# A hybrid encoder step on one core: the last convolution tile's copies on two queues, the parameters turned first, one split moved

## The chip, the cores and the metric

One core of a Trainium2 chip runs the whole step as one program. The metric is the device time in microseconds; a program is run several times and the median counts. The trace and its page come from one profiled execution.

## The reference, cut to what matters

One inference step of two layers over 512 prompt frames and 32 frames of a running stream, 1024 channels, float32. Layer 0 mixes by attention and gated linear attention, layer 1 by a convolution module, and each is followed by a squared-ReLU MLP behind its own RMSNorm:

```
h = rms_norm(x, norm_mix_g[0]) @ w_in_ab        # 3088 columns: q, k, v, two gates, rank-16 part
x = x + merge(attention(h), gla(h)) @ w_out_ab
x = x + square(relu(rms_norm(x, norm_ffn_g[0]) @ w_up)) @ w_down
u = rms_norm(x, norm_mix_g[1]) @ c_w_pw1 + b1   # 2048 columns
u = u[..., :1024] * sigmoid(u[..., 1024:])      # gated
y = depthwise_conv(u, width 31, causal, per channel) + b_dw
x = x + silu(layer_norm(y)) @ c_w_pw2 + b2
x = x + square(relu(rms_norm(x, norm_ffn_g[1]) @ w_up)) @ w_down
```

The outputs are x and the new caches (keys, values, states, the last 30 gated frames).

## The kernel before

**Layout.** Activations lie with channels on the partitions, eight tiles k of 128 channels by 544 frames. Every projection is cut into units of 256 output columns; unit u reads its 1 MB of weights into one of two buffers, `w_raw[:, u % 2]`. Products are made nearly exact in float32 from halves: ScalarE rounds the weights to `w_h` (L608, `split_hi`), VectorE takes the rest `w_l = w_raw - w_h` (L1514, `split_lo`), and the same is done to x (`x_h`, L637 or L676; `x_l`, L1536 or L1547). TensorE adds w_h x_h, w_h x_l and w_l x_h: 96 matmuls of 128x272 a unit (L1017 in `tile`, L1040 in `together`, L1056 in `by_halves`), into two PSUM slots of two banks each.

**Queues.** Each engine has its own instruction stream, in the order written, and semaphores between them. SP issues all weights: unit u + 2's are asked for as soon as `w_lo` says that unit u is split (L416). GpSimd issues the copies and saves of the middle of the kernel. ScalarE issues two small loads at the start (the norm gains).

**Start.** SP sends x (five transfers, L383 and L384), both first units' weights (L410) and 22 small parameter loads (`load_parameters`, L390 to L404), which all count up `rows_landed`. Among these are `dw_rows` (31 rows of 4 KB, the convolution's weights), six pieces `dw_cross` (6 rows each, the same weights with quarters of their channels turned round) and `cc_rows` (30 rows of 4 KB). TensorE turns x, tile after tile, through four PSUM buffers (L996), which VectorE and ScalarE copy out (L1568, L661; semaphores `x_copied`). Then it runs unit 0 of the input projection in `together` as x_l comes in (with a small turning, L1138, before tile 6), then `parameters()`: it waits for all the parameter loads and turns them, 25 small transposes (L1077 to L1085). VectorE copies them out and spreads them (L1579 to L1591) behind unit 0's scaling (L1609). From unit 2 on, VectorE's norms of q and k set the pace.

**Norm ahead of the convolution.** ScalarE's `norm(2, X_MIX1)` takes the square root (L643) and rounds x (L676); after it comes `split_hi(U_PW1, 0, 1)`, the second gated unit's weights (L608), and then the first gate (L894).

**Convolution.** Eight gated units make eight tiles of `glu`, one each (VectorE, L1912). A tile's 31 taps are shared: VectorE does 11 of them (7 for the last tile, L1929 to L1936), TensorE 20 (24 for the last), as diagonal 32x32 matmuls (`taps`, L1398) in five rounds (six for the last) that read the tile and three copies of it, turned round by 32, 64 and 96 partitions: `glu_rot`. GpSimd makes each copy by two DMAs (L579, L580), six a tile, once the tile is gated (`slot_free[1]`), and `moved[m % 2]` counts them. VectorE adds TensorE's sums (L1961) to its own. For the last tile TensorE first adds the mean of tiles 0 to 3 (`add_mean`, L1414), then does `taps(7)`. ScalarE has by then split the first unit of the second pointwise convolution (U_PW2) and loads its square-root table.

**Keeping the clock.** `keep_clock(n, bank)` (L980) issues n matmuls of 128x256 on ones, whose result nobody reads.

Of the kernel before, what the change touches and what calls it, by code (L numbers as in the profile page):

```python
# [84 lines left out]
def hybrid_kernel(nc, x_prompt, x_sample, cache_a_k, cache_a_v, state_b, cache_c, norm_mix_g, norm_ffn_g,  # L85
# [150 lines left out]
    def width(c):  # L236
# [7 lines left out]
    w_hi, w_lo = sem("w_hi"), sem("w_lo")  # L244
    consts, ones_ready = sem("consts"), sem("ones_ready")
    gains_T, gains_ready = sem("gains_T"), sem("gains_ready")
    r_ready, x_sums, r_rows, r_spread, r_T = (
        sem(n) for n in ("r_ready", "x_sums", "r_rows", "r_spread", "r_T"))

    x_copied = [sem(f"x_copied{n}") for n in range(4)]  # L250
    vec_T = sem("vec_T")
    vec_ready = sem("vec_ready")
    gemm_done = sem("gemm_done")
# [125 lines left out]
    @block.sync  # L379
    def _(sp):  # L380
        xp = x_prompt[0].rearrange("(c p) d -> c p d", p=P)
        for c in range(TT):
            sp.dma_start(x_rows[:, c, :], xp[c]).then_inc(x_landed[c], 16)  # L383
        sp.dma_start(x_rows[0:DEC, TT, :], x_sample[0]).then_inc(x_landed[TT], 16)  # L384

        def load_parameters():
            for at, n, src in ((V_B1, 16, as_rows(c_b_pw1)), (V_BDW, 8, as_rows(c_b_dw)), (V_LNG, 8, as_rows(c_ln_g)),
                               (V_LNB, 8, as_rows(c_ln_b)), (V_B2, 8, as_rows(c_b_pw2)), (V_GB, 2, as_rows(b_gate_b)),
                               (V_ON, 1, b_out_norm_g)):
                sp.dma_start(vec_rows[at:at + n, :], src).then_inc(rows_landed, 16)  # L390
            for at, src in ((V_QG, a_q_norm_g), (V_KG, a_k_norm_g)):
                for b in range(2):
                    sp.dma_start(vec_rows[at:at + 1, b * DA:(b + 1) * DA], src).then_inc(rows_landed, 16)
            sp.dma_start(wlr[:], w_view(w_in_ab[0])[:, :, N_PROJ * P:N_PROJ * P + RANK]).then_inc(rows_landed, 16)
# [7 lines left out]
            sp.dma_start(gate_w[:], b_gate_w_up[0]).then_inc(rows_landed, 16)  # L402
            sp.dma_start(rel, a_rel_bias[0]).then_inc(rows_landed, 16)
            sp.dma_start(state_s[:], state_b[0, 0].rearrange("(a b) k v -> (b k) a v", b=2)).then_inc(rows_landed, 16)  # L404

        def stream(u0, units, source, first=False):

            if first:
                for s in range(2):
                    sp.dma_start(w_raw[:, s], source(s)).then_inc(w_landed[s], 16)  # L410
                load_parameters()
            with sp.Fori(1 if first else 0, units // 2) as i:
                for s in range(2):

                    sp.wait_ge(w_lo, i * 2 + (u0 + s - 1))
                    sp.dma_start(w_raw[:, s], source(i * 2 + s)).then_inc(w_landed[s], 16)  # L416
# [12 lines left out]

        sp.wait_ge(pairs_done, 10)  # L430
        stream(U_OUT, 4, columns(w_out_ab[0]))
        ffn(0, U_FFN0)

        stream(U_PW1, 8, columns(c_w_pw1[0]))
        stream(U_PW2, 4, columns(c_w_pw2[0]))
        ffn(1, U_FFN1)

        yp = y_prompt[0].rearrange("(c p) d -> p c d", p=P)
        for k in range(KT):
            sp.wait_ge(y_stage, 2 * (k + 1))  # L440
# [8 lines left out]
    def _(pool):  # L449
# [123 lines left out]
        for m in range(KT):  # L573

            pool.wait_ge(slot_free[1], m + (tile0(U_PW1) // 2 + 1))
            pool.wait_ge(taps_done, m + 1)
            for j in range(1, ROTS):
                at = P - j * (P // ROTS)
                pool.dma_start(glu_rot[0:at, m % 2, j - 1, :], glu[P - at:P, m, 0:PAD + SEQ]).then_inc(moved[m % 2], 16)  # L579
                pool.dma_start(glu_rot[at:P, m % 2, j - 1, :], glu[0:P - at, m, 0:PAD + SEQ]).then_inc(moved[m % 2], 16)  # L580

        pool.wait_ge(edges_out, 2)
        pool.dma_start(cc_prompt[0, 0], ccn[0]).then_inc(stored, 16)
# [6 lines left out]
    def _(act):  # L590
# [6 lines left out]

        for at, src in ((V_MIX, norm_mix_g), (V_FFN, norm_ffn_g)):
            act.dma_start(vec_rows[at:at + 16, :], as_rows(src)).then_inc(gains_landed, 16)

        def split_hi(u, i, d):

# [50 lines left out]
        act.activation(no_use[:], eps[:], ACT.Sqrt)  # L653
        act.wait_ge(gains_ready, 1)
        for k in range(KT):
            hi_gain(0, x_h, k, V_MIX, x_copied[k % 4], k // 4 + 1)
            if k == 1:
                split_hi(0, 0, 0)
                for late in (6, 7):
                    act.wait_ge(gemm_done, late + 1)  # L660
                    act.activation(resid[:, late, :], flat(late % 4)[:, 0:TOK], ACT.Copy).then_inc(x_copied[late % 4], 1)  # L661
                    act.wait_ge(x_copied[late % 4], 2)
        for n, c in enumerate((3, 4)):
            if n:

# [218 lines left out]
                    last(u)  # L884

        ffn(0, U_FFN0, lambda u: phase(u, 4, squares_of(2, u)))
        norm(2, X_MIX1)


# [16 lines left out]

        act.wait_ge(glu_edges, 7)

        split_hi(U_PW1, 0, 1)
        with act.Fori(0, KT // 2 - 1) as i:  # L910
            for s in range(2):
                gate(i, s)
# [7 lines left out]
        gate(KT // 2 - 1, 1)  # L920

        split_hi(U_PW2, 0, 1)
        act.activation(no_use[:], eps[:], ACT.Sqrt)

        def cv_deviation(c):
# [47 lines left out]
    def _(pe):  # L973
# [12 lines left out]
        pe.transpose(ps[:, 4, 0:V_B1], vec_rows[0:V_B1, :], ident[0:V_B1, 0:V_B1]).then_inc(gains_T, 1)  # L986
        pe.wait_ge(gains_ready, 1)
        for k in range(KT):
            if k >= 4:
                pe.wait_ge(x_copied[k % 4], 1)  # L990
            for c in range(TT + 1):
                if k == 0:
                    keep_clock((0, 14, 6, 2, 2)[c], 6)
                    pe.wait_ge(x_landed[c], 16)
                M = width(c)
                ins = pe.transpose(flat(k % 4)[:, c * P:c * P + M], x_rows[0:M, c, k * P:(k + 1) * P],  # L996
                                   ident[0:M, 0:M])
            ins.then_inc(gemm_done, 1)

# [73 lines left out]


        def parameters():
            pe.wait_ge(rows_landed, 16 * 23)
            pe.transpose(ps[:, 7, 0:V_N], vec_rows[:], ident[0:V_N, 0:V_N]).then_inc(vec_T, 1)  # L1077
            for k in range(KT):
                ins = pe.transpose(ps[:, 7, V_N + k * CONV:V_N + (k + 1) * CONV], dw_rows[:, k * P:(k + 1) * P], ident[0:CONV, 0:CONV])
# [52 lines left out]
        def x_ready(k):  # L1132
            if k == KT - 2:

                pe.wait_ge(r_spread, 1)
                for c in range(TT + 1):
                    M = width(c)
# [1 line left out]
                ins.then_inc(r_T, 1)  # L1139
            pe.wait_ge(xl_ready, X_MIX0 + k + 1)  # L1140

        for n in range(4):
            pe.wait_ge(x_copied[n], 2)
        together(0, 0, x_h, x_l, x_ready)
        parameters()
        for u in range(1, U_ATT - 1):
            if u == 2:
                pe.wait_ge(vec_ready, 1)
# [234 lines left out]
        def taps(m):  # L1383
# [4 lines left out]
            pe.wait_ge(moved[s], (m // 2 + 1) * 96)  # L1388

            if m:  # L1390
                pe.wait_ge(conv_step, m * STEPS)
# [86 lines left out]
    def _(dve):  # L1478
# [86 lines left out]

        for k in range(KT - 2):
            dve.wait_ge(gemm_done, k + 1)
            dve.tensor_copy(resid[:, k, :], flat(k % 4)[:, 0:TOK]).then_inc(x_copied[k % 4], 1)  # L1568
        split_lo(0, 0, 0)
        for k in range(KT):  # L1570
            dve.wait_ge(x_copied[k % 4], k // 4 + 1)
            lo_gain(k, X_MIX0, x_l, x_h, V_MIX)
            if k == KT - 3:
                dve.wait_ge(std_ready, 1)
# [2 lines left out]
        def parameters():  # L1577
# [5 lines left out]
            dve.tensor_copy(w_dw[:].rearrange("p k c -> p (k c)"), ps[:, 7, V_N:V_N + KT * CONV])  # L1583
            dve.tensor_copy(dw_rot[:].rearrange("p k c -> p (k c)"), ps[:, 7, V_N + KT * CONV:V_N + KT * (CONV + CROSS)])
            dve.wait_ge(vec_T, 3)
            dve.tensor_copy(cc_T[:].rearrange("p k c -> p (k c)"), ps[:, 6, 0:KT * PAD]).then_inc(vec_ready, 1)

            near = 384 + NREL - 1
# [47 lines left out]
        for u in range(U_ATT):  # L1636
# [3 lines left out]
                copy_rows(3)  # L1640
            split_lo(0, 0, u + 1)
            if u == 0:
                dve.wait_ge(r_ready, 1)
            for m in range(2):
                if 2 <= u < 6:
# [433 lines left out]
```

## Time and profile before

| | us |
|---|---|
| median of 3 runs (lowest, highest) | 1371.54 (1370.0, 1373.36) |
| the profiled execution | 1374.85 |
| its span, first to last instruction | 1373.1 |
| TensorE busy | 1344.9 (98%) |
| VectorE busy | 703.2 (51%) |
| ScalarE busy | 472.7 (34%) |
| mean granted clock of TensorE | 0.993 of full |
| its chain of work, share of TensorE | 90% |

The span is that of the engines' instructions, the execution's time has some 1.75 us around it. TensorE's busy time includes slow matmuls and those of `keep_clock`, so 98% busy does not mean that all of it is needed. A row of the timeline gives the start, the duration, the engine (PE is TensorE, PEld its weight loads, DVE VectorE, ACT ScalarE, POOL GpSimd; a q behind the name is the engine's queue of issues), the line, and in brackets how long the engine stood idle before it and who released it.

### The profile page before, as it was taken

The numbers are of one execution on the slowest core, as the hardware profiler recorded it, in microseconds if no ns is written. First come the engines' busy times: TensorE is split into PE (matmuls) and PEld (weight loads), VectorE is DVE, ScalarE is ACT, GpSimd is POOL, SyncE is SP. The second block draws the span as 40 slices with busy tenths as digits, with TensorE's granted clock in tenths as the row PEclk, the third lists the DMA queues.
The fourth block names the chain that finished last, engine by engine and source line by source line (L and its number), as shares of the span: only waits on it lengthen the run. The fifth ranks groups of instructions, "written<-read, shape, count | busy, mean of one in ns | idle before, by whom it ended". The sixth has DMA issues, their size and how long they took to land.

```text
span 1373.1 us, 27650 instructions
## 1 busy us (share of the span) xinstructions
PE 1344.9 (98%) x11649; PEld 1274.7 (93%) x11649; DVE 703.2 (51%) x1028; ACT 472.7 (34%) x792; POOL 86.5 (6%) x145
## 2 busy tenths in 40 slices
PE   8999999999999999999999999989999999999998
PEld 7998888779999999999999888858999999999998
DVE  5693568575544334334324788877544334334322
ACT  4221556434333223123122544445433223223111
POOL 4001100001100000000011111101100000000000
PEclk9999999999999999999999999999999999999999
DMA  7223300222222222222221433302222221222221
GB/s 253 80 92 106 119 27 2 95 72 93 82 83 82 92 92 92 92 85 74 96 84 62 112 110 106 104 16 69 93 93 92 93 92 61 95 90 92 92 78 50
DMA packets 107293, 119.90 MB, mean 87 GB/s; under 512 B 4435, under 2 KB 103358, under 8 KB 106943
## 3 DMA queue, kind: packets, MB, share of 16 engines
q1 hardware_dynamic: 102783, 101.50, 23.1%
q0 software_dynamic: 4352, 17.02, 4.2%
q8 instruction: 72, 1.18, 0.3%
q14 instruction: 22, 0.18, 0.0%
q10 hardware_dynamic: 64, 0.02, 0.0%
HBM read 104.66 MB, written 7.21 MB: 81 GB/s over the span
## 4 chain that ended last, share of the span: by engine, by line
PE 90%; DVE 5%; ACT 2%; issue 2%; DMA 1%; POOL 0%; SPq 0%; DVEq 0%; ACTq 0%; POOLq 0%
PE ps L1017 70%; PE ps L1173 4%; PE ps L1398 3%; PE ps L1040 3%; DVE rstd L1613 2%; PE ps L1190 1%; PE ps L1284 1%; PE ps L980 1%; PE ps L1223 1%; PE ps L1207 1%; PE ps L1056 1%; PE ps L1002 1%; DVE w_l L1514 1%; PE ps L1438 1%; DMA x_rows<-in_x_sample 1%
## 5 line engine op out<-in xcount | busy, mean ns | idle before, releaser
L608 ACT ACTIVATE w_h<-w_raw 128x2048 fp32r<-128x2048 f32 x92 | 175.4, 1907 | 276.4 <-PE ps L1017 272.9
L1514 DVE TENSOR_TENSOR w_l<-w_raw,w_h 128x2048 fp32r<-128x2048 f32 x92 | 210.8, 2291 | 102.8 <-ACT w_h L608 102.7
L1017 PE MATMUL ps<-x_h,w_h 128*128 128x272 f32 x1152 | 242.0, 292 | 2.4 <-ACT sig L894 1.5
L1017 PE MATMUL ps<-x_l,w_h 128*128 128x272 f32 x1152 | 238.6, 288 | 0.0
L1017 PE MATMUL ps<-x_h,w_l 128*128 128x272 f32 x1152 | 238.2, 288 | 0.0
L1017 PE MATMUL ps<-xf_h,w_h 128*128 128x272 f32 x1024 | 212.9, 289 | 0.0
L1017 PE MATMUL ps<-xf_l,w_h 128*128 128x272 f32 x1024 | 211.2, 287 | 0.0
L1017 PE MATMUL ps<-xf_h,w_l 128*128 128x272 f32 x1024 | 210.9, 287 | 0.0
L1017 PEld LDWEIGHTS ps<-x_h,w_h 128*128 128x128 f32 x1152 | 180.9, 189 | 9.1 <-issue 8.7
L1017 PEld LDWEIGHTS ps<-x_l,w_h 128*128 128x128 f32 x1152 | 182.6, 189 | 0.0
L1017 PEld LDWEIGHTS ps<-x_h,w_l 128*128 128x128 f32 x1152 | 180.7, 188 | 0.0
L1017 PEld LDWEIGHTS ps<-xf_l,w_h 128*128 128x128 f32 x1024 | 161.5, 188 | 0.0
L1017 PEld LDWEIGHTS ps<-xf_h,w_h 128*128 128x128 f32 x1024 | 159.9, 188 | 0.2
L1017 PEld LDWEIGHTS ps<-xf_h,w_l 128*128 128x128 f32 x1024 | 159.8, 188 | 0.0
L1861 DVE TENSOR_TENSOR resid<-ps,resid 128x544 f32 x64 | 46.3, 724 | 200.6 <-PE ps L1017 199.7
L870 ACT ACTIVATE relu<-relu 128x544 f32<-128x544 f32 x64 | 42.2, 659 | 239.9 <-DVE relu L1879 239.9
L1017 PE MATMUL ps<-odd_h,w_h 128*128 128x272 f32 x512 | 106.8, 290 | 0.0
L1017 PE MATMUL ps<-odd_l,w_h 128*128 128x272 f32 x512 | 105.6, 287 | 0.0
L1017 PE MATMUL ps<-odd_h,w_l 128*128 128x272 f32 x512 | 105.5, 287 | 0.0
L1879 DVE SCALAR_TENSOR_TENSOR relu<-ps,xn 128x544 f32<-128x544 f32 x64 | 46.2, 722 | 89.6 <-PE ps L1017 89.5
L1017 PEld LDWEIGHTS ps<-odd_l,w_h 128*128 128x128 f32 x512 | 80.8, 188 | 0.0
L1017 PEld LDWEIGHTS ps<-odd_h,w_l 128*128 128x128 f32 x512 | 79.9, 188 | 0.0
(278 smaller groups left out, 1653.5 us busy)
## 6 DMA issues: line engine op xcount, KB each, us to landing
w_raw<-in_w_ffn_up SPq DMA_DIRECT2D x32, 1024.0 KB, 5.3
w_raw<-in_w_ffn_down SPq DMA_DIRECT2D x32, 1024.0 KB, 5.1
w_raw<-in_w_in_ab SPq DMA_DIRECT2D x12, 1024.0 KB, 5.3
w_raw<-in_c_w_pw SPq DMA_DIRECT2D x12, 1024.0 KB, 6.1
w_raw<-in_w_out_ab SPq DMA_DIRECT2D x4, 1024.0 KB, 5.5
glu_rot<-glu POOLq DMA_DIRECT2D x16, 203.2 KB, 5.4
resid_scratch<-resid POOLq DMA_DIRECT2D x1, 2176.0 KB, 8.1
resid<-resid_scratch POOLq DMA_DIRECT2D x1, 2176.0 KB, 9.0
```

The lines of the kernel that those rows point to most:

```text
L608: act.activation(w_h[s][:], w_raw[:, s], ACT.Copy).then_inc(w_hi, 1)
L870: act.activation(relu2[:, m, :], relu[:, m, :], ACT.Square).then_inc(relu2_done, 1)
L980: pe.matmul(ps[:, bank, 0:2 * P], any_bits[:, 0:P], any_bits, start=True, stop=True)
L1002: ins = pe.matmul(dst[:, a, :], w[:], src[:, a * n:(a + 1) * n], start=start, stop=stop)
L1017: ins = pe.matmul(ps[:, 2 * m + t, 0:HALF], a[s][:, k, w], b[:, k, t * HALF:(t + 1) * HALF], start=(k == 0 and q == 0), stop=(k == KT - 1 ...
L1040: ins = pe.matmul(ps[:, 2 * m + t, 0:HALF], a[s][:, k, w], b[:, k, t * HALF:(t + 1) * HALF], start=(k == 0 and q == 0), stop=(k == KT - 1 ...
L1173: ins = pe.matmul(ps[:, 2 * m + t, 0:HALF], a[u % 2][:, k, m * P:(m + 1) * P], b[:, k, t * HALF:(t + 1) * HALF], start=(k == 0 and q == 0) ...
L1398: ins = pe.matmul(ps[to, 4 + r, :], diag[rows, s, tap, :], src, start=(n == 0), stop=(n == rounds(m) - 1))
L1514: dve.tensor_tensor(w_l[s][:], w_raw[:, s], w_h[s][:].bitcast(F32), ALU.subtract).then_inc(w_lo, 1)
L1613: dve.reciprocal(rstd[:, 0:TOK], sumsq[:]).then_inc(rstd_ready, 1)
L1861: dve.tensor_tensor(r, slot(m), r, ALU.add).then_inc(slot_free[m], 1)
L1879: dve.scalar_tensor_tensor(out=halves(relu[:, m, :]), in0=slot(m), scalar=0.0, in1=halves(r_tok), op0=ALU.max, op1=ALU.mult).then_inc(slot ...
```

## The change

Four things are done:

1. **Last tile's copies.** GpSimd issues only three of the last tile's six copies; ScalarE issues the other three, behind its split of U_PW2's first unit, with their own semaphore `moved_last`. SP's weights for U_PW2 + 2 and the one after wait for all six. TensorE runs eight `keep_clock` matmuls between `add_mean(3)` and `taps(7)`.
2. **Parameters.** The eleven loads of vectors go to ScalarE's queue. SP sends dw_rows, dw_cross and cc_rows between the first and the second unit's weights, and the other four (`load_late_parameters`) behind the second, counted by `late_rows`. TensorE turns the parameters ahead of unit 0, with a wait for 19 loads, and then runs eight `keep_clock` matmuls; VectorE handles them ahead of unit 0's scaling and waits there for the late four.
3. **Three PSUM buffers for x** instead of four, since the parameters' turnings use the last two banks.
4. **Split.** `split_hi(U_PW1, 0, 1)` stands ahead of `norm(2, X_MIX1)`.

```diff
         def load_parameters():
-            for at, n, src in ((V_B1, 16, as_rows(c_b_pw1)), ... (V_ON, 1, b_out_norm_g)):
-                sp.dma_start(vec_rows[at:at + n, :], src).then_inc(rows_landed, 16)
-            (4 more of a_q_norm_g, a_k_norm_g; wlr)
             sp.dma_start(dw_rows[:], c_w_dw[0]).then_inc(rows_landed, 16)
...
             sp.dma_start(cc_rows[:], cache_c[0, 0]).then_inc(rows_landed, 16)
-            (gate_w, rel, state_s)
+        def load_late_parameters():
+            (wlr, gate_w, rel, state_s, each .then_inc(late_rows, 16))
...
                 for s in range(2):
                     sp.dma_start(w_raw[:, s], source(s)).then_inc(w_landed[s], 16)
-                load_parameters()
+                    (load_parameters, load_late_parameters)[s]()
...
-        stream(U_PW2, 4, columns(c_w_pw2[0]))
+        stream(U_PW2, 2, columns(c_w_pw2[0]))
+        sp.wait_ge(moved[(KT - 1) % 2], KT // 2 * 96 - 48)
+        sp.wait_ge(moved_last, 48)
+        stream(U_PW2 + 2, 2, columns(c_w_pw2[0], 512))
...  (GpSimd)
                 pool.dma_start(glu_rot[0:at, ...], glu[P - at:P, m, ...]).then_inc(moved[m % 2], 16)
-                pool.dma_start(glu_rot[at:P, ...], glu[0:P - at, m, ...]).then_inc(moved[m % 2], 16)
+                if m < KT - 1:
+                    pool.dma_start(glu_rot[at:P, ...], glu[0:P - at, m, ...]).then_inc(moved[m % 2], 16)
...  (ScalarE)
+        (at the start: the eleven loads of vec_rows, .then_inc(rows_landed, 16))
-            hi_gain(0, x_h, k, V_MIX, x_copied[k % 4], k // 4 + 1)
+            hi_gain(0, x_h, k, V_MIX, x_copied[k % 3], k // 3 + 1)
...
+        split_hi(U_PW1, 0, 1)
         norm(2, X_MIX1)
         act.wait_ge(glu_edges, 7)
-        split_hi(U_PW1, 0, 1)
...
         split_hi(U_PW2, 0, 1)
+        act.wait_ge(slot_free[1], KT - 1 + (tile0(U_PW1) // 2 + 1))
+        act.wait_ge(taps_done, KT)
+        for j in range(1, ROTS):
+            at = P - j * (P // ROTS)
+            act.dma_start(glu_rot[at:P, (KT - 1) % 2, j - 1, :], glu[0:P - at, KT - 1, 0:PAD + SEQ])\
+                .then_inc(moved_last, 16)
         act.activation(no_use[:], eps[:], ACT.Sqrt)
...  (TensorE)
-            if k >= 4:
-                pe.wait_ge(x_copied[k % 4], 1)
+            if k >= 3:
+                pe.wait_ge(x_copied[k % 3], k // 3)
...
-            pe.wait_ge(rows_landed, 16 * 23)
+            pe.wait_ge(rows_landed, 16 * 19)
...
-        for n in range(4):
-            pe.wait_ge(x_copied[n], 2)
+        parameters()
+        for n in range(2):
+            pe.wait_ge(x_copied[n], 3)
+        keep_clock(8, 0)
         together(0, 0, x_h, x_l, x_ready)
-        parameters()
...
         for k in range(4):
             add_mean(k)
+        pe.wait_ge(slot_free[1], tile0(U_PW2) // 2)
+        keep_clock(8, 2)
         taps(KT - 1)
...  (VectorE)
+            dve.wait_ge(late_rows, 16 * 4)      (in parameters())
...
             if u == 0:
+                parameters()
                 dve.wait_ge(r_ready, 1)
...
-            if u == 0:
-                parameters()
```

## Rows read from the trace of the kernel before

**Rows 1.** The page, chain of work that ended last, by engine.

```profile
PE 90%; DVE 5%; ACT 2%; issue 2%; DMA 1%; POOL 0%; SPq 0%; DVEq 0%; ACTq 0%; POOLq 0%
```

**Rows 2.** Timeline of the start: start us, us, engine, line, operation.

```profile
4.74 5.57 SPq L390 DMA_DIRECT2D vec_rows<-in_c_b_pw  x1
...
13.97 0.43 SPq L395 DMA_DIRECT2D dw_rows<-in_c_w_dw  x1
...
19.25 0.46 SPq L401 DMA_DIRECT2D cc_rows<-in_cache_c  x1
...
11.51 1.44 ACT L637 ACTIVATE x_h<-resid,vecs 128x544 fp32r<-128x544 f32 x2 [8.27 <-DVE resid L1568]
...
13.12 1.91 ACT L608 ACTIVATE w_h<-w_raw 128x2048 fp32r<-128x2048 f32 x1 [0.17 <-DMA w_raw<-in_w_in_ab]
...
18.25 0.61 PE L1040 MATMUL ps<-x_h,w_h 128*128 128x272 f32 x2 [2.28 <-DVE x_l L1536]
```

**Rows 3.** Windows: busy us of each engine, granted clock, DMA share, GB/s.

```profile
18.25:21.83 3.58, 3.58 (x16) 3.58 (x17) 3.33 (x5) 3.55 (x7) 0.00 (x0) 0.53 0.22 68
...
883.70:889.20 5.50, 5.50 (x162) 2.83 (x160) 3.95 (x6) 3.40 (x3) 1.22 (x3) 1.00 0.20 63
...
897.40:902.40 5.00, 4.95 (x96) 2.17 (x97) 1.84 (x3) 0.00 (x0) 0.00 (x0) 0.50 0.00 0
```

**Rows 4.** Chain and VectorE timeline at the ends of units 0 and 1.

```profile
32.90 0.07 PE ps L1077
...
34.58 12.28 PE ps L1017 x96
...
46.88 0.73 DVE L1609 TENSOR_TENSOR proj<-ps,xn 128x544 f32<-128x544 f32 x1 [5.30 <-PE ps L1017]
```

**Rows 5.** Timeline around the last tile's copies and taps.

```profile
887.98 0.52 POOL L579 DMA_DIRECT2D glu_rot<-glu  x1 [14.62 <-DVE glu L1912]
...
890.51 0.52 POOL L580 DMA_DIRECT2D glu_rot<-glu  x1
...
889.22 4.15 PE L1414 MATMUL ps<-cv,mean_d 128*128 128x288 f32 x16
...
897.45 1.08 PE L1398 MATMUL ps<-glu,diag 32*32 32x512 f32 x4 [4.08 <-DMA glu_rot<-glu]
...
906.35 0.69 DVE L1961 TENSOR_TENSOR rstd<-ps,rstd 128x512 f32<-128x512 f32 x1 [7.04 <-PE ps L1398]
...
910.68 1.04 PE L980 MATMUL ps<-ones 128*128 128x256 bf16 x8
```

**Rows 6.** Timeline of the norm ahead of the gated units.

```profile
744.68 0.71 ACT L643 ACTIVATE sumsq<-ps,eps 128x544 f32<-128x544 f32 x1 [2.69 <-PE ps L1002]
...
759.21 1.90 ACT L608 ACTIVATE w_h<-w_raw 128x2048 fp32r<-128x2048 f32 x1
...
765.27 0.49 PE L1017 MATMUL ps<-x_h,w_h 128*128 128x272 f32 x2 [1.52 <-ACT sig L894]
```

**Rows 7.** DMA issues, us to landing: last tile's longest copies, first tile's.

```profile
glu_rot<-glu POOLq DMA_DIRECT2D x2, 203.2 KB, 5.9
...
glu_rot<-glu POOLq DMA_DIRECT2D x2, 203.2 KB, 3.6
```

**Rows 8.** DMA packets in 5:6, 17:18, 22:22.5 and 22.5:23 us.

```profile
DMA packets 107, 0.38 MB, mean 377 GB/s; under 512 B 14, under 2 KB 15, under 8 KB 107
...
DMA packets 60, 0.04 MB, mean 36 GB/s; under 512 B 54, under 2 KB 54, under 8 KB 60
...
DMA packets 57, 0.01 MB, mean 28 GB/s; under 512 B 50, under 2 KB 57, under 8 KB 57
...
DMA packets 134, 0.07 MB, mean 147 GB/s; under 512 B 7, under 2 KB 132, under 8 KB 134
```

**Rows 9.** VectorE timeline: unit 0's scalings, last parameter operation.

```profile
32.25 1.41 DVE L1609 TENSOR_TENSOR proj<-ps,xn 128x544 f32<-128x544 f32 x2 [4.76 <-PE ps L1040]
...
36.14 0.18 DVE L1591 COPY proj<-proj 8x65 f32<-8x65 f32 x1
```

More of the change, by code:

```diff
@@ L246, in hybrid_kernel @@
     gains_T, gains_ready = sem("gains_T"), sem("gains_ready")
+    moved_last = sem("moved_last")
+    late_rows = sem("late_rows")
     r_ready, x_sums, r_rows, r_spread, r_T = (
         sem(n) for n in ("r_ready", "x_sums", "r_rows", "r_spread", "r_T"))
-    x_copied = [sem(f"x_copied{n}") for n in range(4)]
+    x_copied = [sem(f"x_copied{n}") for n in range(3)]
     vec_T = sem("vec_T")
@@ L386, in load_parameters @@
         def load_parameters():
-            for at, n, src in ((V_B1, 16, as_rows(c_b_pw1)), (V_BDW, 8, as_rows(c_b_dw)), (V_LNG, 8, as_rows(c_ln_g)),
-                               (V_LNB, 8, as_rows(c_ln_b)), (V_B2, 8, as_rows(c_b_pw2)), (V_GB, 2, as_rows(b_gate_b)),
-                               (V_ON, 1, b_out_norm_g)):
-                sp.dma_start(vec_rows[at:at + n, :], src).then_inc(rows_landed, 16)
[L391 to L394, printed above, removed]
             sp.dma_start(dw_rows[:], c_w_dw[0]).then_inc(rows_landed, 16)
@@ L401, in load_parameters @@
             sp.dma_start(cc_rows[:], cache_c[0, 0]).then_inc(rows_landed, 16)
-            sp.dma_start(gate_w[:], b_gate_w_up[0]).then_inc(rows_landed, 16)
-            sp.dma_start(rel, a_rel_bias[0]).then_inc(rows_landed, 16)
-            sp.dma_start(state_s[:], state_b[0, 0].rearrange("(a b) k v -> (b k) a v", b=2)).then_inc(rows_landed, 16)
+        def load_late_parameters():
+            sp.dma_start(wlr[:], w_view(w_in_ab[0])[:, :, N_PROJ * P:N_PROJ * P + RANK]).then_inc(late_rows, 16)
+            sp.dma_start(gate_w[:], b_gate_w_up[0]).then_inc(late_rows, 16)
+            sp.dma_start(rel, a_rel_bias[0]).then_inc(late_rows, 16)
+            sp.dma_start(state_s[:], state_b[0, 0].rearrange("(a b) k v -> (b k) a v", b=2)).then_inc(late_rows, 16)
         def stream(u0, units, source, first=False):
@@ L579, in _ @@
                 pool.dma_start(glu_rot[0:at, m % 2, j - 1, :], glu[P - at:P, m, 0:PAD + SEQ]).then_inc(moved[m % 2], 16)
-                pool.dma_start(glu_rot[at:P, m % 2, j - 1, :], glu[0:P - at, m, 0:PAD + SEQ]).then_inc(moved[m % 2], 16)
+                if m < KT - 1:
+                    pool.dma_start(glu_rot[at:P, m % 2, j - 1, :], glu[0:P - at, m, 0:PAD + SEQ])\
+                        .then_inc(moved[m % 2], 16)
         pool.wait_ge(edges_out, 2)
@@ L599, in _ @@
             act.dma_start(vec_rows[at:at + 16, :], as_rows(src)).then_inc(gains_landed, 16)
+        for at, n, src in ((V_B1, 16, as_rows(c_b_pw1)), (V_BDW, 8, as_rows(c_b_dw)), (V_LNG, 8, as_rows(c_ln_g)),
+                           (V_LNB, 8, as_rows(c_ln_b)), (V_B2, 8, as_rows(c_b_pw2)), (V_GB, 2, as_rows(b_gate_b)),
+                           (V_ON, 1, b_out_norm_g)):
+            act.dma_start(vec_rows[at:at + n, :], src).then_inc(rows_landed, 16)
+        for at, src in ((V_QG, a_q_norm_g), (V_KG, a_k_norm_g)):
+            for b in range(2):
+                act.dma_start(vec_rows[at:at + 1, b * DA:(b + 1) * DA], src).then_inc(rows_landed, 16)
         def split_hi(u, i, d):
@@ L660, in _ @@
                     act.wait_ge(gemm_done, late + 1)
-                    act.activation(resid[:, late, :], flat(late % 4)[:, 0:TOK], ACT.Copy).then_inc(x_copied[late % 4], 1)
-                    act.wait_ge(x_copied[late % 4], 2)
+                    act.activation(resid[:, late, :], flat(late % 3)[:, 0:TOK], ACT.Copy).then_inc(x_copied[late % 3], 1)
+                    act.wait_ge(x_copied[late % 3], 3)
         for n, c in enumerate((3, 4)):
@@ L995, in _ @@
                 M = width(c)
-                ins = pe.transpose(flat(k % 4)[:, c * P:c * P + M], x_rows[0:M, c, k * P:(k + 1) * P],
+                ins = pe.transpose(flat(k % 3)[:, c * P:c * P + M], x_rows[0:M, c, k * P:(k + 1) * P],
                                    ident[0:M, 0:M])
@@ L1133, in x_ready @@
             if k == KT - 2:
+                pe.wait_ge(x_copied[2], 2)
                 pe.wait_ge(r_spread, 1)
@@ L1387, in taps @@
             pe.wait_ge(slot_free[1], m + (tile0(U_PW1) // 2 + 1))
-            pe.wait_ge(moved[s], (m // 2 + 1) * 96)
+            if m < KT - 1:
+                pe.wait_ge(moved[s], (m // 2 + 1) * 96)
+            else:
+                pe.wait_ge(moved[s], (m // 2 + 1) * 96 - 48)
+                pe.wait_ge(moved_last, 48)
             if m:
@@ L1567, in _ @@
             dve.wait_ge(gemm_done, k + 1)
-            dve.tensor_copy(resid[:, k, :], flat(k % 4)[:, 0:TOK]).then_inc(x_copied[k % 4], 1)
+            dve.tensor_copy(resid[:, k, :], flat(k % 3)[:, 0:TOK]).then_inc(x_copied[k % 3], 1)
         split_lo(0, 0, 0)
         for k in range(KT):
-            dve.wait_ge(x_copied[k % 4], k // 4 + 1)
+            dve.wait_ge(x_copied[k % 3], k // 3 + 1)
             lo_gain(k, X_MIX0, x_l, x_h, V_MIX)
@@ L1585, in parameters @@
             dve.wait_ge(vec_T, 3)
+            dve.wait_ge(late_rows, 16 * 4)
             dve.tensor_copy(cc_T[:].rearrange("p k c -> p (k c)"), ps[:, 6, 0:KT * PAD]).then_inc(vec_ready, 1)
```

## The prediction

> **What bounds the kernel now.** The page comes first: its chain of work that ended last belongs to TensorE for nine tenths [rows 1]. A microsecond counts here only where TensorE is late for its next dense stretch. The change touches three such places, so I read each in the timeline, engine by engine, and then asked the windows for the granted clock there.
>
> The first is the start. TensorE has turned x by 15.97 us (its next row starts at 18.25 after 2.28 us idle), then waits for VectorE's x_l [rows 2]. It comes back slow: from 18.25 to 21.83 the mean granted clock is 0.53, practically the 1.2 GHz level, and 16 matmuls take 3.58 us [rows 3]; at the full 2.4 GHz, as in unit 1, 96 take 12.28 [rows 4], so 16 would take 2.0. Unit 0 ends at 32.90, the parameters' 25 turnings follow until 34.58, and unit 1 starts [rows 4].
>
> The second is the gap ahead of the last tile's taps. GpSimd issues that tile's six copies from 887.98 on, half a microsecond each; the last was issued at 890.51 and TensorE waited for it until 897.45, 4.08 us idle; its mean work before had ended at 889.22 + 4.15 = 893.37 [rows 5]. The clock fell there too: 0.50 over the 5 us after, and VectorE, which had been done for 7.04 us, got the sums at 906.35 [rows 3, 5].
>
> The third is the norm ahead of the gated units [rows 6].
>
> **The copies.** Before, the 1 MB of a later unit's weights goes out beside them, and the longest copies took 5.9 us to landing; for the first tile, whose copies start almost 3 us behind the weights, the same ones took 3.6 [rows 7]. After, SP holds the weights back until the copies are in, GpSimd issues three copies and ScalarE three. GpSimd's third is issued 2 x 0.52 us behind 887.98, at 889.0; with 3.6 us it lands at 892.6. ScalarE's three start when its unit is gated, about 887.7, and are no later. TensorE has mean work until 893.37 anyway, and then eight clock matmuls, 1.04 us in the row of the same eight [rows 5], 0.95 of it their own: taps can start at 894.3, so the landing has 1.7 us to spare. At full clock five rounds took 5.45 us (the stretch of tile 6 [rows 3]); the last tile has six, 6.54. They end at 900.85, and VectorE starts its sums at 900.95 instead of 906.35: **5.4 us less**, some 3.15 from the start and 2.25 from the clock. VectorE is free at 906.35 - 7.04 = 899.31, 1.6 us ahead, so it does not take over. Bounds: landings of 5.9 us as before give 894.9, 0.6 us lost; 0 more is to be had by faster ones, since the clock matmuls stand in the way. ScalarE's three issues and its table load are covered by its next wait, which ends only behind VectorE's sums. The held weights land near 898, and their unit is split only after unit 0 of this projection, which starts when the whole normalisation is done. Nothing else stands behind SP's two waits: all SP does later is weights.
>
> One rule of the Trainium skill speaks against the second queue (DMA: Bandwidth & Descriptors, "Issuing engines are not separate DMA queues"): all issuers share the same 16 engines, so a second one saves issue time only. The trace agrees that issue time counts (six issues end at 891.03, three at about 889.5), and the sum above takes its gain from that and from the held weights, not from bandwidth.
>
> **The parameters.** Removed: 1.68 us between unit 0 and unit 1 (32.90 to 34.58 [rows 4]). Added: the same turnings ahead of unit 0, a wait for 19 transfers, eight clock matmuls, and three PSUM buffers for x instead of four. The third buffer suffices: a tile's copy runs while the next is turned, so the buffer of three tiles ago is free a tile ahead.
>
> So all hangs on when the 19 transfers are in. Eleven small ones move to ScalarE's queue; at SP's 0.3 to 0.45 us each they cost it about 5 us at the start, where it has 8.27 us idle before 11.51 [rows 2]. The other eight are dw_rows, six pieces of dw_cross and cc_rows. Before, SP gave them out from 13.97 to 19.71, behind both units of weights; SP also stood 5.57 us in the first small one [rows 2]. After, they follow the first unit alone: issued between 4 and 10 us, or by 15 if SP stands likewise. They are then moved behind the first weights, which land at 13.10 (ScalarE's wait [rows 2]). And dw_rows goes slowly: between 17 and 18 us, with nothing else moving, there are 60 packets, 54 of them under 512 B and 6 of 4 KB [rows 8]. While x came in, 92 of 4 KB went over 16 engines in a microsecond (107 less 15) [rows 8]; six is one engine's rate. Its 31 rows are therefore a 31 / 6 = 5.2 us job. Behind them on that engine are its share of dw_cross (50 small packets in the half microsecond from 22.0) and two rows of cc_rows (the two large ones from 22.5 on) [rows 8]: 0.7 + 0.3 us. The landing lag is the same as for the weights, so the rows are in at 13.1 + 6.2 = 19.3; the engine may be done with the weights before the slowest one, and I take **19.0**, against TensorE's 15.97. From below: 18.2, if the engine is free 1.1 us ahead of that landing. From above: 20.4: before, the rows were given out at 13.97 and done by 22.0, so they may have taken up to 1.4 us more than 5.2 behind the second weights.
>
> The Trainium skill has this as a rule (DMA: Bandwidth & Descriptors, "Why a DMA increments its semaphore by 16 and not by 1"): a hardware-issued transfer runs on the largest number of engines up to 16 that divides its outer dimension, and always on the lowest-numbered. For 31 rows that is one; the trace agrees, with its 6 packets a microsecond. Were the rows spread over all sixteen, the sum would be that of rival (a) below.
>
> Against the start at 18.25 that gives: resumption 0.75 us later; eight clock matmuls in front of unit 0, 0.95; the turnings only change place; at the end of unit 0 nothing stands between it and unit 1 any more, which must wait for VectorE's first scaling (0.70 us, begun 0.65 before the end [rows 4, 9]): 0.1. The clock: idle 3.0 us instead of 2.28. 2.28 us idle was followed by 3.58 slow, 4.08 by 5.0 [rows 2, 3, 5], in between 4.2; 0.6 us more at half speed costs 0.25. **Together 2.05 us more** (1.25 to 3.5 with the bounds).
>
> Cover elsewhere: VectorE's share (its last operation ends at 36.32, some 2.2 us behind the turnings it waits for) moves to 27.5, where it had 4.76 us idle [rows 9], if the four late transfers are in by then; they are issued behind the second weights, by about 18, and should land by 24. The second weights lose their early place: behind dw_rows on that one engine they land near 22. Their split on ScalarE and VectorE takes 4.2 us and TensorE needs it at 34 [rows 4]: 8 us to spare, less what VectorE's queue adds. Does the 2.05 us pass through? VectorE waited 5.30 us for unit 1's end at 46.88 [rows 4], and its bound stretch begins from that, so yes.
>
> **The earlier split.** ScalarE had 2.69 us idle before 744.68, the split takes 1.91 and fits with 0.8 to spare. It was at 759.21 and its result is due with the gate, and the gate waits for unit 0 and a table load, not for it: TensorE's 1.52 us of idle are ended by the sigmoid [rows 6]. **0 us**; worst case about 1, should the split push the square root.
>
> **Sum.** -5.4 + 2.05 + 0 = -3.35 us on a profiled execution of 1374.85 (span 1373.1, 1.75 around it). The median shown is 3.3 lower, 1371.54; the same step gives **1368.2**.
>
> **Rivals.** (a) The rows are in before 15.97. Then the turnings fill the gap, the clock never falls, unit 0 starts at 15.97 + 1.68 + 0.95 = 18.6 and ends 13.07 us later (14.65 less 1.58 of slow clock) at 31.7, unit 1 starts at 31.8 instead of 34.58: -2.8, in all -8.2, **1363.3**. For it: the small packets are quick. Against it: one engine needs 5.2 us for dw_rows and can't start before 11. 0.17.
>
> (b) The turnings all run at the lower level, and the slow stretch of 4.2 us only follows, over the clock matmuls and unit 0. The turnings take 1.68 x 0.8 = 1.35 us more: -2.0, **1369.5**. For it: both slow stretches of the rows ended inside long runs of matmuls, none inside turnings. Against it: nothing in the rows says that turnings are different. 0.18.
>
> (c) Slower: the rows land no sooner than before, about 24 (last large packets after 22.5, and the lag), because SP's stand of 5.57 us or the one engine delays them in their new place too. TensorE then stands 8 us: 5.75 + 0.95 + 0.1 + 0.6 of clock = 7.4, less 5.4 = +2.0, **1373.5**. It decides from a landing at 22.3 on. Against it: the packets' order above. 0.08.
>
> (d) The copies still take their 6.7 us: they land at 895.7, taps begin 1.4 us later, gain 4.0: **1369.6**; with the clock lost too, about 1372. 0.12.
>
> My forecast 0.45, on its own 1367 to 1370. 0.3% is 4.1 us, about what this measurement can tell: the forecast stands just inside. Faster by more: (a) and some 0.2 of the forecast (rows by 18.4, or the last bits of the copies): 0.37. Slower by more: 0.08. Within: 0.55. Range: 1363.2, the foot of (a), to 1371.8, above (d).
>
> **What would show it.** Start: TensorE idle from 16 to 19, released by a transfer, clock 0.5 for about 4 us, unit 1 at 36.6. No idle and unit 1 at 31.8 is (a); slow beyond 4 us of dense work is (b); a start after 22.3 is (c). Taps of the last tile: start 8 clock matmuls behind 893.4 in old time, no wait, clock 1.00, 6.5 us long. The norm unchanged but for the split's place. I am wrong if dw_rows does not hold one engine, or if a stage between 47 and 250 us absorbs the start's delay.

## The result, and the profile after

The changed kernel takes 1374.62 us (median of 20 runs, 1373.16 to 1376.08) against 1371.78 for the kernel before on the same chip (20 runs, 1369.17 to 1374.26). The ratio is 1.0019, 95% interval 1.0013 to 1.0026: **slower by 0.2%, 2.6 us**, where 3.3 us less was predicted and the range ended at 1371.8. That is within the 0.3% that counts here as no change, but on the slower side, outside the range. The profiled execution took 1374.62 us (span 1372.9), which is 0.2 less than the profiled execution of before (1374.85). So one profiled execution and the median tell different stories here.

**The start.** First the chain of waits of the kernel after, from 15 to 41 us (start, us, what); it answers to [rows 2, 4].

```profile
10.43 10.03 DMA cc_rows<-in_cache_c
20.46 0.04 issue
20.51 0.40 PE ps L1094
20.91 0.99 PE ps L1096 x8
21.90 0.83 PE ps L1099 x8
22.73 0.87 PE ps L1102 x8
23.61 1.82 PE ps L997 x8
25.43 9.83 PE ps L1057 x72
35.26 0.61 PE ps L1156 x5
35.87 2.48 PE ps L1057 x18
...
38.40 0.47 issue
38.86 0.74 DVE proj L1635
...
39.73 1.37 PE ps L1034 x9
```

and two rows of TensorE's timeline at the end of unit 0:

```profile
38.67 0.41 PE L1057 MATMUL ps<-x_h,w_l 128*128 128x272 f32 x2
39.73 0.49 PE L1034 MATMUL ps<-x_h,w_h 128*128 128x272 f32 x2 [0.65 <-DVE proj L1635]
```

TensorE stands until the last of the 19 transfers is in at 20.46, turns the parameters for 3.1 us (1.68 before), runs eight clock matmuls for 1.82, and starts unit 0 at 25.43. The chain leaves TensorE at 38.35, where the first half of unit 0's result is ready for VectorE; the last matmul of unit 0 ends at 39.08. Unit 1 starts at 39.73, behind VectorE's first scaling, 5.15 us later than in [rows 4]. Three PSUM buffers for x suffice: turning it takes 5.56 us before and after. The windows of the same kernel (busy us of each engine, granted clock, DMA share, GB/s) show the clock from the end of x on:

```profile
16.80:20.50 3.70, 0.00 (x0) 0.00 (x0) 3.70 (x5) 3.61 (x6) 0.00 (x0) 0.96 0.33 65
20.50:23.60 3.10, 3.09 (x26) 2.88 (x27) 1.88 (x3) 3.07 (x6) 0.00 (x0) 0.50 0.56 142
23.60:27.00 3.40, 3.40 (x17) 2.96 (x17) 2.95 (x4) 2.19 (x3) 1.72 (x2) 0.50 0.70 243
27.00:28.00 1.00, 1.00 (x10) 1.00 (x9) 1.00 (x1) 0.00 (x0) 0.15 (x1) 0.98 0.65 279
...
889.45:894.40 4.95, 4.95 (x160) 2.60 (x128) 3.45 (x6) 1.65 (x1) 1.17 (x3) 1.00 0.04 11
899.40:905.90 6.50, 6.50 (x193) 3.65 (x192) 5.09 (x7) 0.00 (x0) 0.00 (x0) 1.00 0.49 164
```

All of the turnings are at 0.50, the 1.2 GHz level, and so are the 3.4 us behind them.

**Why the rows were late.** SP's timeline in the kernel after:

```profile
3.90 0.66 SPq L389 DMA_DIRECT2D dw_rows<-in_c_w_dw  x1
...
10.43 0.76 SPq L395 DMA_DIRECT2D cc_rows<-in_cache_c  x1
11.23 1.76 SPq L407 DMA_DIRECT2D w_raw<-in_w_in_ab  x1
13.04 5.72 SPq L398 DMA_DIRECT2D wlr<-in_w_in_ab  x1
```

SP gave all eight out between 3.90 and 11.2, as predicted; its stand of 5.7 us moved to the first late transfer, where nobody waits for it. What was late is the one engine that works on `dw_rows`: from 13 to 18 us it passed only 4 or 5 packets of 4 KB in each microsecond, where the sum had 6. The DMA packets in 13:14, 15:16 and 18:19:

```profile
DMA packets 41, 0.05 MB, mean 49 GB/s; under 512 B 5, under 2 KB 37, under 8 KB 41
...
DMA packets 346, 0.37 MB, mean 370 GB/s; under 512 B 0, under 2 KB 341, under 8 KB 346
...
DMA packets 40, 0.02 MB, mean 20 GB/s; under 512 B 37, under 2 KB 37, under 8 KB 40
```

The large ones are the last figure less the one before it: 4, 5 and 3. In 15:16 the second unit's weights go beside them, 341 smaller packets on all engines. The last three of `dw_rows` pass between 18 and 18.5, at the 6 a microsecond of the sum; the 37 small ones come behind them, then the two large ones of `cc_rows`. From about 11.6 (11 large packets in 11.5:12, none in 10.5:11.5) to 19.6 us the engine was at it: some 7 us for `dw_rows` and 1 for the rest.

**The copies.** The timeline around the last tile, answering to [rows 5]:

```profile
892.97 1.91 ACTq L938 DMA_DIRECT2D glu_rot<-glu  x3
893.23 1.53 POOL L580 DMA_DIRECT2D glu_rot<-glu  x3 [14.64 <-DVE glu L1937]
894.47 4.15 PE L1437 MATMUL ps<-cv,mean_d 128*128 128x288 f32 x16
...
898.46 1.04 PE L997 MATMUL ps<-ones 128*128 128x256 bf16 x8
...
899.37 0.37 SPq L413 DMA_DIRECT2D w_raw<-in_c_w_pw  x1
...
906.06 0.69 DVE L1986 TENSOR_TENSOR rstd<-ps,rstd 128x512 f32<-128x512 f32 x1 [1.50 <-PE ps L1421]
```

and of the copies (first and last issue; us to landing):

```profile
L938 ACTq DMA_DIRECT2D glu_rot<-glu x3: 616/617/623, 893.0 to 894.3; - x3
...
glu_rot<-glu ACTq DMA_DIRECT2D x1, 203.2 KB, 5.0
```

Mean work, clock matmuls and taps follow each other without a wait, the taps take 6.50 us at clock 1.00, and VectorE gets the sums at 906.06: 13.1 us after the first copy, against 906.35 - 887.98 = 18.4 in [rows 5]. Everything here is 5.25 us late from the start, and still the sums come 0.3 us sooner. The margin is thin: ScalarE's last copy, given out at 894.3, is in at 899.2, 0.6 us behind the end of the mean work and about 0.2 ahead of the taps; the clock matmuls cover that gap. Against that one execution the gain is 906.35 + 5.25 - 906.06 = 5.5 us, where 5.4 was predicted.

### The profile page after: what moved, and what is told of

Its sections match the earlier page's. It is cut to its first block, busy times and chain, and to the rows that moved or that the text cites. A ratio compares the mean times of both kernels' runs of the same rounds, so it can differ in the third digit from the quotient of the medians.

```text
span 1372.9 us, 27674 instructions
## 1 busy us (share of the span) xinstructions
PE 1347.1 (98%) x11665; PEld 1276.1 (93%) x11665; DVE 702.7 (51%) x1028; ACT 472.4 (34%) x792; POOL 84.4 (6%) x142
## 4 chain that ended last, share of the span: by engine, by line
PE 91%; DVE 4%; ACT 2%; issue 1%; DMA 1%; SPq 1%; POOL 0%; ACTq 0%; DVEq 0%; POOLq 0%
PE ps L1034 71%; PE ps L1192 4%; PE ps L1421 3%; PE ps L1057 3%; DVE rstd L1639 2%; PE ps L997 1%; PE ps L1209 1%; PE ps L1303 1%; PE ps L1242 1%; PE ps L1226 1%; PE ps L1019 1%; DMA cc_rows<-in_cache_c 1%; PE ps L1073 1%; DVE w_l L1539 1%; PE ps L1463 1%
```

## The experiments

All ratios are to the kernel before on the same chip. There were eleven runs, two of them of the kernel before itself.

**1. The kernel before again, and each part alone.**

> The kernel before, unchanged, profiled and timed once more. The profiled execution shown took 1374.85 us, above every one of its 20 timed ones (1369.17 to 1374.26, median 1371.78). Theory A (that execution was unlucky: one or both of its slow stretches of TensorE's clock, at 18.25 and 897.45 us, is often absent or shorter): this profile ends 2 to 4 us sooner, and the difference lies in a stretch with granted clock near 0.5, at the start or at the last tile's taps. Theory B (the profile costs some 3 us of its own, everywhere): the profile again takes 1374 to 1375 us and the same stretches are slow. Timed: ratio 1.000 within 0.001 either way.

> Only the last tile's part: three copies issued by ScalarE, later weights held back, eight clock matmuls ahead of the taps. From the two traces this part gives back 5.5 us (unit times 5.2 us later at tile 6, 0.3 earlier at the last tile's sums). If the gap and its slow clock are there in every execution of the kernel before: 5.0 to 5.5 us faster, ratio 0.9960. If the clock falls there only in some executions: about 3.2 to 4.5 us faster, 0.997 to 0.9975.

The copies' part: three of the six copies on ScalarE's queue, two units' weights held back, eight clock matmuls.

> Only the start: parameters' loads reordered and turned ahead of unit 0, three buffers for x, eight clock matmuls. From the two profiled executions: unit 1 starts 5.2 us later (39.7 instead of 34.6), ratio 1.0038. If the start of the kernel before is usually quicker than in the profiled execution (its clock falls at 18.25 only sometimes, worth up to 1.6 us, or x lands sooner), the timed loss is larger: 6 to 8.5 us, 1.0045 to 1.006, since the measured whole is +2.8 and the copies gain at most 5.5.

The parameters' part, with its eight clock matmuls.

> Only the split of the second gated unit's weights moved ahead of the norm. It fills idle time of ScalarE and nobody waits for its result: 0 us, ratio 1.0000 within 0.0007. Rival: it delays the square root or the loads and costs 1 us or more, which would explain part of what the sum of the two traces leaves open.

```diff
+        split_hi(U_PW1, 0, 1)
         norm(2, X_MIX1)
...
-        split_hi(U_PW1, 0, 1)
         with act.Fori(0, KT // 2 - 1) as i:
```

| kernel | median us | ratio, 95% | profiled: us, clock |
|---|---|---|---|
| before again | 1371.22 | 0.9999 [0.9989, 1.0009] | 1372.86, 0.995 |
| copies only | 1368.81 | 0.9980 [0.9971, 0.9989] | 1368.99, 0.996 |
| parameters only | 1377.98 | 1.0052 [1.0039, 1.0065] | 1377.91, 0.994 |
| split only | 1372.42 | 1.0000 [0.9989, 1.0011] | 1374.67, 0.993 |

In us at 1371.9: copies -2.7 (-4.0 to -1.5), parameters +7.1 (5.4 to 8.9), split 0. Their sum, +4.4, is 1.8 above the whole change's, which the three intervals allow. So the copies give half of what was predicted, and the new start costs more than three times as much as predicted.

**2. The rows of the taps in two transfers, and the start without its clock matmuls.** The first of the two edits, made on the parameters' part alone and on the whole change:

```diff
-            sp.dma_start(dw_rows[:], c_w_dw[0]).then_inc(rows_landed, 16)
+            sp.dma_start(dw_rows[0:16], c_w_dw[0, 0:16]).then_inc(rows_landed, 16)
+            sp.dma_start(dw_rows[16:CONV], c_w_dw[0, 16:CONV]).then_inc(rows_landed, 16)
...
-            pe.wait_ge(rows_landed, 16 * 19)
+            pe.wait_ge(rows_landed, 16 * 20)
```

> The start part alone, and dw_rows loaded by two transfers of 16 and 15 rows instead of one of 31. Theory (the 31 rows of 4 KB run on one DMA engine, 0.2 us each, and hold the parameters back until 20.5): now the rows are in at 15 to 16 us, before x is turned at 16.5 to 16.8; the parameters are turned at once, 1.7 us at full clock, TensorE's granted clock does not fall, unit 0 starts near 19.3 and unit 1 near 33 instead of 39.7: 1.5 to 2 us sooner than in the kernel before (34.6 to 35.2), and timed about 2 to 3 us faster than it, ratio 0.998 to 0.9985. Rival (the small pieces of dw_cross or SP's issue times hold the rows): in at 18 to 20 us, unit 1 at 37 to 39, slower than before by 3 us or more.

The second, on the parameters' part alone:

```diff
-        keep_clock(8, 0)
         together(0, 0, x_h, x_l, x_ready)
```

> The start part alone, without its eight clock matmuls ahead of unit 0. They ran at half clock for 1.8 us. If they only stand in the way: unit 0 starts 1.8 us sooner, but the slow stretch of 3.4 us then covers unit 0's matmuls instead, at a cost of 0.9 of it; unit 1 starts 0.9 to 1.0 us sooner (38.8 to 39.0). If they bring the clock back: unit 1 no sooner, within 0.2 us.

> The whole changed kernel with dw_rows in two transfers. The start's gain of 1.5 to 2 us and the copies' 2.7 to 5.5: 4.5 to 7 us faster than the kernel before, ratio 0.995 to 0.9967, and 7 to 10 us faster than the changed kernel. If the rows are not what holds the start: as the changed kernel, 1.002.

| kernel | median us | ratio, 95% |
|---|---|---|
| parameters, rows spread | 1373.26 | 1.0006 [0.9992, 1.0019] |
| parameters, no clock matmuls | 1374.64 | 1.0023 [1.0011, 1.0035] |
| whole change, rows spread | 1368.83 | 0.9968 [0.9953, 0.9982] |

The timeline of TensorE with the rows spread, parameters only:

```profile
17.46 0.29 PE L1083 MATMUL ps<-ident,vec_rows 85*128 85x85 f32 x1 [1.17 <-DMA cc_rows<-in_cache_c]
17.68 0.68 PE L1085 MATMUL ps<-ident,dw_rows 31*128 31x31 f32 x8
...
19.28 1.45 PE L986 MATMUL ps<-ones 128*128 128x256 bf16 x8
20.39 0.80 PE L1046 MATMUL ps<-x_h,w_h 128*128 128x272 f32 x2
```

and in the whole change with the rows spread:

```profile
16.57 0.29 PE L1095 MATMUL ps<-ident,vec_rows 85*128 85x85 f32 x1
...
18.39 1.05 PE L998 MATMUL ps<-ones 128*128 128x256 bf16 x8
19.92 0.48 PE L1058 MATMUL ps<-x_h,w_h 128*128 128x272 f32 x2 [0.48 <-DVE x_l L1562]
```

The same bytes in two transfers of 16 and 15 rows are in 3 us sooner (17.4) or before TensorE asks at all: from 14 us on the first of these kernels has 4 packets of 4 KB left (2 in 14:15, 2 in 15:16), where the kernel after had 23; the rows go 0.68 us through TensorE instead of 1.06, at full clock, and timed 4.6 of the 5.2 thousandths are gone. The rule of the Trainium skill that the prediction used (DMA: Bandwidth & Descriptors, "Why a DMA increments its semaphore by 16 and not by 1") says that the outer dimension sets the number of engines; this experiment changes that dimension, at the price of one transfer more, and the time follows. Without the clock matmuls the late rows stay late, and unit 1 starts at 39.07 instead of 39.90; timed, the step is 1.0052 (five runs) to 1.0023, so these matmuls bring nothing behind a stall of 3.7 us. That they cost more than the 0.8 us of the profile is not shown: the two intervals almost touch. The third kernel beats both: 0.3% faster than before, and 0.5% faster than the change by the ratio of their ratios.

The first kernel missed its expectation: TensorE still waited 1.17 us for the last transfer, the clock fell at 19.8 us for 3.4 us, and unit 1 started at 35.44, not near 33. Timed it is no faster than the kernel before, where 2 to 3 us were expected. The third came out at the slow end of what was expected of it (0.995 to 0.9967).

**3. The two halves of the copies' part, the kernel before a third time, and the best version without the clock matmuls ahead of unit 0.** Queue only keeps ScalarE's three copies and the clock matmuls and drops what holds the weights back (this edit and the next are shown against the changed kernel; start and split are those of before):

```diff
-        stream(U_PW2, 2, columns(c_w_pw2[0]))
-        sp.wait_ge(moved[(KT - 1) % 2], KT // 2 * 96 - 48)
-        sp.wait_ge(moved_last, 48)
-        stream(U_PW2 + 2, 2, columns(c_w_pw2[0], 512))
+        stream(U_PW2, 4, columns(c_w_pw2[0]))
```

> Half of the copies' part: the last tile's six copies on two queues and the eight clock matmuls, the last two units' weights as early as in the kernel before; start and split as before. The whole part gave -2.7 us timed. Theory, that the clock matmuls cover what the weights beside the copies still cost: landings of 5 to 6 us from 888.7 to 889 on end at 894 to 895, mean work ends near 893 and the clock matmuls 1 us later, so the taps wait 0 to 1 us and the clock stays 1.00: 1369 to 1370, ratio 0.998 to 0.999. Rival, that the gain is that of the held weights: landings stay at 6.7 us, taps wait 1.5 us or more and the clock falls: 1371 to 1372.

Hold only leaves all six copies on GpSimd:

```diff
-                if m < KT - 1:
-                    pool.dma_start(glu_rot[at:P, m % 2, j - 1, :], ...)
+                pool.dma_start(glu_rot[at:P, m % 2, j - 1, :], ...)
...
-        sp.wait_ge(moved[(KT - 1) % 2], KT // 2 * 96 - 48)
-        sp.wait_ge(moved_last, 48)
+        sp.wait_ge(moved[(KT - 1) % 2], KT // 2 * 96)
```

> The other half: all six copies stay on GpSimd, the weights of the last two units go out behind them, and the eight clock matmuls stand in front of the taps. The last copy is issued some 2.5 us behind the first, near 890.2, and with 3.6 to 4.5 us it is in at 893.8 to 894.7 against 893.8 to 894 for the end of the clock matmuls: a wait of 0 to 0.9 us, clock 1.00, 1368.8 to 1370. Rival, that the issue time of six on one queue is what costs: wait over 1.5 us, 1371 or more.

> The whole change with the rows of the taps in two transfers of 16 and 15 rows, and without the eight clock matmuls ahead of unit 0 (those ahead of the last tile's taps stay). With them the same kernel gave 1368.83, 0.9968 of the kernel before, and no slow stretch at the start. Theory A, that they only cost their 0.95 us where nothing is waited for: unit 0 starts 0.9 to 1.0 us earlier, the clock stays 1.00, 0.996, near 1368. Rival B, that VectorE's first x_l sets the start of unit 0 (idle of 0.48 us there in that kernel): 0 to 0.5 us earlier, and the gap costs a slow stretch of 3.4 us, which is 1.7 us: 0.997 to 0.998.

> The kernel before once more, for a third profile of it. If its slow stretches around the last tile's copies are the same in every execution: 6.8 us at half clock between 895 and 903 as in the first profile, and 1374 to 1375. If they vary from execution to execution: 3.4 us there as in the second, or another number, and a time of the profiled execution that goes with the slow time in all (13.6 us slow gave 1372.9, 20.5 gave 1374.9). Ratio 0.999 to 1.001.

| kernel | median us | ratio, 95% | profiled: us, clock |
|---|---|---|---|
| queue only | 1372.22 | 1.0005 [0.9990, 1.0020] | 1376.08, 0.991 |
| hold only | 1368.71 | 0.9974 [0.9960, 0.9988] | 1370.89, 0.993 |
| spread, no clock matmuls | 1367.84 | 0.9972 [0.9959, 0.9985] | 1370.85, 0.993 |
| before, third time | 1370.34 | 0.9991 [0.9976, 1.0005] | 1371.42, 0.995 |

The gain of the copies' part comes with the weights that are held back; the second queue adds nothing to it. Both halves have the clock matmuls, so held weights without them are not tested; in hold only the last copy is in 0.6 us behind the mean work, as in the change. DMA issues and their landing (us) with the second queue and the weights beside it:

```profile
glu_rot<-glu POOLq DMA_DIRECT2D x1, 203.2 KB, 6.0
glu_rot<-glu ACTq DMA_DIRECT2D x1, 203.2 KB, 7.7
glu_rot<-glu ACTq DMA_DIRECT2D x1, 135.5 KB, 6.5
...
glu_rot<-glu POOLq DMA_DIRECT2D x1, 67.8 KB, 7.4
```

and with one queue and the weights held back:

```profile
glu_rot<-glu POOLq DMA_DIRECT2D x2, 203.2 KB, 3.0
glu_rot<-glu POOLq DMA_DIRECT2D x2, 135.5 KB, 2.6
glu_rot<-glu POOLq DMA_DIRECT2D x2, 67.8 KB, 2.7
```

The queue-only kernel issues sooner and lands no sooner: its taps start 9.23 us after its first copy, and the seven profiles with the old copies have 8.1 to 9.5. In the hold-only kernel that is 6.2, in the whole part 6.4 to 6.5; both run from mean work through the clock matmuls into the taps without a wait, and both reach the next landmark, VectorE's first split of weights behind the convolution, the same 4.5 us sooner than the second profile of before. So rival "issue time costs" fell, and so did my expectation that queue only would reach 1369 to 1370: the wait was 2.7 us, not 0 to 1. It bears out the rule that was weighed in the prediction (the Trainium skill, DMA: Bandwidth & Descriptors, "Issuing engines are not separate DMA queues"), which calls the issue time that a second queue saves usually small beside the transfer itself; the prediction had held against it that six issues against three count, and they did not.

The clock matmuls ahead of unit 0 can't be told apart from none once the rows are early (0.9968 and 0.9972). Neither theory of that run could be read from its profile, since the clock had fallen at 11.9 us already, ahead of the code that differs. Nor can either be told from hold only (0.9974): with the rows early the new start costs nothing that shows, and what it gains, if anything, is lost in the intervals.

**4. What the clock does when nothing is changed.** Windows of 895.5 to 902.5 us, where the last tile's taps begin, in the second profile of the kernel before:

```profile
895.50:902.50 7.00, 6.26 (x152) 3.64 (x164) 2.81 (x4) 0.00 (x0) 0.00 (x0) 0.76 0.01 2
```

and in the third:

```profile
895.50:902.50 7.00, 6.17 (x192) 3.66 (x192) 3.91 (x6) 0.00 (x0) 0.00 (x0) 1.00 0.02 5
```

The first profile has 0.50 over the same taps [rows 3]. Reading the stages in this way gives the time at half clock, us:

| profile of | start | attention, near 140 | last tile's taps | near 930 |
|---|---|---|---|---|
| before | 3.4 | 6.8 | 6.8 | 3.4 |
| before again | 3.4 | 3.4 | 3.4 | 3.4 |
| before, third | 6.8 | 3.4 | 0 | 3.4 |
| copies only | 3.4 | 6.8 | 0 | 0 |
| hold only | 13.7 | 3.4 | 0 | 0 |
| after | 6.8 | 6.8 | 0 | 0 |
| whole, rows spread | 0 | 6.8 | 0 | 0 |
| the same, no clock matmuls | 13.7 | 3.4 | 0 | 0 |

The time at half clock at one place differs between executions of one kernel: 6.8, 3.4 and 0 us at the last tile's taps in the three profiles of before. Of seven profiles with the old copies (the three of before, split only, and the three with the parameters' part alone) three fell at the last tile's taps, after 3.81, 3.84 and 4.08 us idle, and four stayed at 1.00, after 2.68 to 3.53 us idle; what differed was the landing of the last copy (6.4 to 6.7 us against 5.3 to 6.1). The stretch near 930 is in all seven of these and in none of the six with clock matmuls ahead of the last taps, and it costs nothing that shows: from VectorE's sums to the end of the span it is 466.8 us in the first profile of before (1373.1 - 906.35) and 466.8 in copies only. The timed runs show the same spread: 93 of the kernel before go from 1367.56 us at mean clock 0.999 to 1377.79 at 0.989, 0.91 us for each 0.001 (correlation -0.90).

## Why the prediction was wrong

**The copies: the mechanism right, their worth at the median half.** The path of that paragraph came true (taps behind the clock matmuls, no wait, full clock, no cost of SP's two waits). Its landing did not: 4.6 us behind GpSimd's first copy, with 1.7 to spare, were 6.0 with some 0.2 to spare, and the clock matmuls hid it. Nor did the second queue's issue time, to which the sum gave part of the gain, bring any: hold only is as fast without it. The step that failed is "5.4 us less, some 3.15 from the start and 2.25 from the clock", carried to the median by "the same step gives 1368.2". The first profile of before was one of the three in seven with the clock fallen there, in its longest form (6.8 us), and its copies took the longest of all. Against the third profile the gain is 2.0 us (taps without a wait instead of 8.2 us behind the first copy), against the second 4.5, against the first 5.5. Over all seven profiles with the old copies, GpSimd's first copy to the end of the span takes 481.5 to 485.2 us, 483.1 on average, against 479.7 with the weights held back: 3.5 us. Timed it is 2.7 (1.5 to 4.0). The page of the profile gave a warning beforehand: mean clock 0.993, 3.3 us above the median.

**The rows: 6.2 us of one engine were 8.** The mechanism held, the size was off: "its 31 rows are therefore a 31 / 6 = 5.2 us job". The 6 rows a microsecond were read where nothing else moved; in their new place the second unit's weights go beside them, the engine passed 4 or 5, and the rows took some 7 us. The 1.0 us behind them came out as worked out. That the engine began near 11.6, not at 13.1, gave back part of it. The rows were in at 20.46: 1.5 us past the 19.0 and just past the upper bound of 20.4. That the single transfer was the cause is shown by spreading it.

**The clock: rival (b) was right, but for its time.** "0.6 us more at half speed costs 0.25" failed. The turnings ran wholly at the lower level (+1.4), and 3.4 us of half clock followed, over clock matmuls (1.82 instead of 0.95) and the head of unit 0. Against the expected 2.05 us the start lost 5.15: resumption 20.51 - 18.25 = 2.26, turnings 3.10 - 1.68 = 1.42 more than the place they left, clock matmuls 1.82, unit 0 shorter by 1.0 (25.43 to 39.08, against 18.25 to 32.90), and the wait for VectorE at its end 0.65, where the sum had 0.1: it began its scaling 0.2 us ahead of unit 0's end, not 0.65. The terms add up to 5.15. Timed, the parameters' part costs 7.1 (5.4 to 8.9, five runs). Its mean clock in those runs was 0.9936 against 0.9949 of the kernel before on that chip, 3.6 us more at half clock, which is about what the 5.15 already hold; where the other 2 us are, or whether there are any, stays open.

**Rival (a) was there to be had.** With the rows spread, the turnings fill the gap and the clock did not fall in that execution. Unit 1 starts at 33.72 instead of 34.58, not the 31.8 worked out there: x_l was ready only at 19.9, so that VectorE set unit 0's start (18.6 there), and TensorE waited 0.66 us for it again at unit 0's end. **(c)** and **(d)** fell: the rows were in before 22.3, and the slowest copy took 5.0 us, not 6.7.

**The split: 0, as predicted.** Alone it measures 1.0000. VectorE's split of that unit comes 1.2 us sooner, and no landmark behind it moves.

**The chances.** "Slower by over 0.3%" got 0.08, and the time ended at +0.2%. Both errors had one sign, and the range did not hold a start of rival (b)'s kind together with copies at their median worth: -2.7 + 5.15 gives +2.45 on 1371.54, 1374.0.

## What to carry to other kernels

Before a gain is read off one profile, compare its mean clock and time with the timed runs: a slow stretch in it is worth its price times how often it occurs. When a dense stretch waits for a small load, look at its outer dimension first; 31 rows in one transfer cost more than 31 rows in two. When copies are late, move other traffic away before adding a queue, and do not expect clock matmuls to help behind a stall: behind one of 3.7 us they brought nothing. Whether they help over a short gap was not tested here.

## What the runs showed of the hardware

- The granted clock varies where the code does not. The old start had 3.4, 3.4 and 6.8 us at half clock in the three profiles of the kernel before, and 13.7 in hold only and queue only, whose start is the old one; there it fell at 12.0 and 11.5 us. Over a whole execution 13.6 to 20.5 us were slow in three profiles of one kernel.
- A slow stretch of 3.4 us cost 1.5 us in the last tile's taps (8.08 us in the second profile of before, 6.58 in the third), and the one near 930 nothing that shows: per microsecond of slow time the 93 timed runs lost 0.33 us on average (0.91 us per 0.001 of clock, which is 2.74 us at half).
- Three copies on each of two queues landed later each (median 3.9 to 4.0 us) than six on one (2.7 in hold only), and the last was in 6.1 to 6.2 us behind the first issue, against 6.0. With 1 MB of weights beside them the medians were 6.4 and 5.2.
- The one engine that moves `dw_rows` passed 6 packets of 4 KB a microsecond with little beside them and 4 or 5 beside a unit's weights.
- A small transfer given out behind large ones held SP for 5.6 to 5.7 us in both kernels, [rows 2] and at 13.04 after: the stand goes with the place in the queue, not with the transfer.
